# Retention heads of a hybrid decoder step: another plan for the paged sample rows, with key products and key sums at other places in the slot

## The reference

```python
z = h @ w_in            # h = RMSNorm(x); ret_q|ret_k|ret_v|ret_gate|diff_q|diff_k|diff_v|diff_gate
# retention, 4 heads, in chunks of 128 rows with a state S:
inner = einsum('bihd,bjhd->bhij', q, k) * dmask
o     = einsum('bhij,bjhe->bihe', inner, v) + einsum('bihd,bhde->bihe', q * q_dec, S)
S     = gamma**L * S + einsum('bjhd,bjhe->bhde', k * k_dec, v)
# differential attention, 4 heads, two softmax maps of 64 dims each:
a = softmax(s1) - lam * softmax(s2);   o = a @ v
# a sample attends to its cache: 32 pages of 128 positions
past_k = cache_k[page_table];  past_v = cache_v[page_table]
y = x + concat(rms(o_ret) * silu(rg), rms(o_diff) * (1 - lam_init) * silu(dg)) @ w_out
```

## Time and profile before

| | |
|---|---|
| median of 3 runs (lowest, highest) | 1890.08 us (1884.31, 1897.64) |
| the profiled execution | 1889.52 us |
| its span | 1887.7 us |
| granted TensorE clock over the span | 0.937 |
| PE busy | 1633.7 us |
| DVE busy | 1138.0 us |
| POOL busy | 1043.9 us |

### The profile page before, as it was taken

The page is one execution under the profiler, slowest core; times in us unless marked ns, Lnnn a source line. Parts: engine busy times, 40 slices in busy tenths (PEclk is TensorE's granted clock), DMA queues, the critical chain, the costliest instruction groups (busy, mean ns, idle before and its releaser), DMA issues. The chain is left out here.

```text
span 1887.7 us, 28473 instructions
## 1 busy us (share of the span) xinstructions
PE 1633.7 (87%) x8308; PEld 1207.1 (64%) x8308; DVE 1138.0 (60%) x1947; ACT 732.8 (39%) x1947; POOL 1043.9 (55%) x1927
## 2 busy tenths in 40 slices
PE   6869889899888968888999988998988975489999
PEld 1247657576666736676877766876776754366886
DVE  2469677676776635776756978665786753125521
ACT  2333223232232323556655655665554653210000
POOL 4658667767666536787456887556578633200000
PEclk9889999999999979999999999999998996689999
DMA  8764576656548341321025222223233013154441
GB/s 292 251 190 131 165 232 196 207 164 213 188 144 277 118 132 60 90 84 51 23 79 154 82 75 66 68 84 101 88 92 112 24 59 120 56 156 144 145 134 58
DMA packets 169628, 241.00 MB, mean 128 GB/s; under 512 B 15393, under 2 KB 82090, under 8 KB 169458
## 3 DMA queue, kind: packets, MB, share of 16 engines
q1 hardware_dynamic: 137970, 205.55, 34.5%
q10 hardware_dynamic: 28432, 25.21, 4.2%
q0 software_dynamic: 3072, 8.43, 1.1%
HBM read 211.37 MB, written 27.76 MB: 127 GB/s over the span
## 5 line engine op out<-in xcount | busy, mean ns | idle before, releaser
L589 POOL TENSOR_TENSOR s_ring<-s_ring,s_q_row 128x1024 f32<-128x1024 f32 x128 | 316.0, 2485 | 48.7 <-DMA s_ring<-in_cache_k 45.1
L1064 PE MATMUL s_z<-g_w_hi,s_h_hi 128*128 128x512 f32 x512 | 228.4, 446 | 22.3 <-DVE s_h_lo L963 15.8
L1606 PE MATMUL s_z<-g_w_hi,s_h_hi 128*128 128x512 f32 x512 | 225.1, 440 | 24.8 <-DVE s_h_lo L1501 14.3
L1066 PE MATMUL s_z<-g_w_hi,s_h_lo 128*128 128x512 f32 x512 | 206.8, 404 | 0.0
L1065 PE MATMUL s_z<-g_w_lo,s_h_hi 128*128 128x512 f32 x512 | 205.4, 401 | 0.0
L1608 PE MATMUL s_z<-g_w_hi,s_h_lo 128*128 128x512 f32 x512 | 205.2, 401 | 0.0
L1607 PE MATMUL s_z<-g_w_lo,s_h_hi 128*128 128x512 f32 x512 | 204.5, 399 | 0.0
L1350 ACT ACTIVATE s_p<-s_sc,s_neg_max 128x1024 f32<-128x1024 f32 (+4 forms) x192 | 167.0, 874 | 77.0 <-DVE s_neg_max L1531 49.6
L1655 PE MATMUL s_o<-s_v,s_aT 128*128 128x128 f32 x1088 | 168.7, 298 | 15.5 <-ACT s_aT L1331 15.4
L1655 PEld LDWEIGHTS s_o<-s_v,s_aT 128*128 128x128 f32 x1088 | 147.2, 204 | 52.8 <-ACT s_aT L1331 49.2
L963 DVE TENSOR_TENSOR s_h_lo<-g_hT,s_h_hi 128x512 fp32r<-128x512 f32 x128 | 159.0, 1281 | 6.6 <-ACT s_h_hi L854 4.0
(11 more groups left out here) (241 smaller groups left out, 3561.0 us busy)
## 6 DMA issues: line engine op xcount, KB each, us to landing
s_ring<-in_cache_k SPq DMA_DIRECT2D x256, 256.0 KB, 3.0
s_ring<-in_cache_v SPq DMA_DIRECT2D x256, 256.0 KB, 2.9
w_raw<-in_w_in SPq DMA_DIRECT2D x8, 2048.0 KB, 9.8
x_in<-in_x_prompt SPq DMA_DIRECT2D x16, 512.0 KB, 7.0
s_table<-c_rope_ret ACTq DMA_DIRECT2D x64, 128.0 KB, 3.4
s_w_raw<-in_w_in ACTq DMA_DIRECT2D x32, 256.0 KB, 3.6
u_scratch<-s_gate POOLq DMA_DIRECT2D x32, 256.0 KB, 2.6
s_u_in<-u_scratch SPq DMA_DIRECT2D x16, 512.0 KB, 4.8
```

Of the source, the lines that this page charges most:

```text
L589: pool.tensor_tensor(slot[:], slot[:], bc(R.q_row[:].unsqueeze(1), [P, 2, 512]), ALU.mult).then_inc(R.keys_times_q, 1)
L1064: pe.matmul(b[:], hi[:, c, :], g.w_hi[:, wc, :], start=(wc == 0), stop=False)
L1066: last = pe.matmul(b[:], lo[:, c, :], g.w_hi[:, wc, :], start=False, stop=(wc == DC - 1))
L1606: pe.matmul(z_bank[:], hi[:, c, :], g.w_hi[:, wc, :], start=(wc == 0), stop=False)
```

## The change

The plan of the retention stage has other slots. `spread` writes out a slot for each pair or quad, from counts. Row 0 has keys in slots 0 to 5 (2, 3, 3, 3, 3, 2) and values in slots 10 to 16. Rows 1 to 4 end at 17, 29, 41 and 53, 12 slots apart; each has its keys in the 12 slots up to its end and its values in seven slots from end+5, one quad a slot and two in the fourth.

POOL's key products go behind `scale_gates` and `finish` in the slot, and wait until DVE has written both low parts of the slot (`half_low`). DVE's key sums and row steps go from ahead of `mask_inner` to behind `next_state`. `row_stat` gets two buffers; so the wait for the stores of the row before is one row more lenient at end+2, and a wait for them stands at `own`, ahead of the write of `row_own`. The differential stage keeps its plan and its order, and shares the last point.

```diff
-        self.row_stat = sb("row_stat", [HC, 2])
+        self.row_stat = [sb(f"row_stat{i}", [HC, 2]) for i in range(2)]
...
         elif s == end + 2:
             dve.wait_ge(R.row_pe, q + 1)
-            if r >= 1:
-                dve.wait_ge(R.row_stored, 32 * r)
+            if r >= 2:
+                dve.wait_ge(R.row_stored, 32 * (r - 1))
...
         if s == R.own[r]:
             dve.wait_ge(R.values_used, NPAIR // 2 * (r + 1))
+            if r >= 1:
+                dve.wait_ge(R.row_stored, 32 * r)
...
-RET_PLAN = [
-    (list(range(0, 9)), 8, [13, 14, 15, 16, 17, 18]),
-    (list(range(11, 21)), 20, [25, 26, 27, 28, 29, 30]),
-    (list(range(23, 33)), 32, [37, 38, 39, 40, 41, 42]),
-    (list(range(35, 45)), 44, [49, 50, 51, 52, 53, 54]),
-    (list(range(47, 57)), 56, [61, 62, 63, 64]),
-]
+def spread(first, counts):
+
+    return [first + i for i, n in enumerate(counts) for _ in range(n)]
+
+
+RET_VALUES = [1, 1, 1, 2, 1, 1, 1]
+RET_PLAN = [(spread(0, [2, 3, 3, 3, 3, 2]), 5, spread(10, RET_VALUES))] + [
+    (spread(end - 11, [2, 2, 2, 2, 1, 1, 1, 0, 1, 1, 1, 2]), end, spread(end + 5, RET_VALUES))
+    for end in (17, 29, 41, 53)]
...
                 if 0 <= s - 1 < TILES:
                     rotate(s - 1)
-                row_keys_pool(pool, R, s)
                 if s % 2 == 0 and 0 <= (s - 2) // 2 < TILES // 2:
                     scale_gates((s - 2) // 2)
                 done = s - RET_LAG - 2
                 if is_block(done) and done % GROUP == GROUP - 1:
                     finish(done // GROUP)
+                if s in R.keys:
+                    pool.wait_ge(half_low, 2 * s + 4)
+                row_keys_pool(pool, R, s)
                 row_store(pool, io, R, s)
...
                 if is_block(c - 1):
                     gate_output(c - 1)
-                row_keys_dve(dve, R, s - 1)
-                row_steps_dve(dve, g, R, s)
                 if is_block(c):
                     mask_inner(c)
...
                 if is_block(c):
                     next_state(c)
+                row_keys_dve(dve, R, s - 1)
+                row_steps_dve(dve, g, R, s)
                 if k < NH and t == NT - 1:
                     for x in range(DC // 2):
                         split_w(k + 1, x)
```

More of the change, by code:

```diff
@@ L609, in row_steps_dve @@
             dve.wait_ge(R.row_pe, q + 1)
-            if r >= 1:
-                dve.wait_ge(R.row_stored, 32 * r)
-            dve.tensor_reduce(R.row_stat[:, 0:1], R.row_bank[0:HC, 0:P], AX, ALU.max).then_inc(R.row_dve, 1)
+            if r >= 2:
+                dve.wait_ge(R.row_stored, 32 * (r - 1))
+            dve.tensor_reduce(R.row_stat[r % 2][:, 0:1], R.row_bank[0:HC, 0:P], AX, ALU.max).then_inc(R.row_dve, 1)
             dve.wait_ge(R.row_dve, d + 2)
-            dve.tensor_scalar(R.row_diag[:], g.ident[0:HC, 0:HC], R.row_stat[:, 0:1], None, ALU.mult
+            dve.tensor_scalar(R.row_diag[:], g.ident[0:HC, 0:HC], R.row_stat[r % 2][:, 0:1], None, ALU.mult
                               ).then_inc(R.row_dve, 1)
@@ L624, in row_steps_dve @@
             dve.wait_ge(R.row_pe, q + 3)
-            dve.tensor_copy(R.row_stat[:, 1:2], R.row_bank[0:HC, 0:1]).then_inc(R.row_dve, 1)
+            dve.tensor_copy(R.row_stat[r % 2][:, 1:2], R.row_bank[0:HC, 0:1]).then_inc(R.row_dve, 1)
         if s == R.own[r]:
             dve.wait_ge(R.values_used, NPAIR // 2 * (r + 1))
+            if r >= 1:
+                dve.wait_ge(R.row_stored, 32 * r)
             dve.tensor_tensor(R.row_own[:].rearrange("p (h e) -> p h e", e=P),
@@ L680, in row_store @@
             pool.wait_ge(R.row_dve, ROW_DVE * (r + 1))
-            pool.dma_start(io["row_stats"][row:row + 1].rearrange("b s k -> (b s) k"), R.row_stat[:]
+            pool.dma_start(io["row_stats"][row:row + 1].rearrange("b s k -> (b s) k"), R.row_stat[r % 2][:]
                            ).then_inc(R.row_stored, 16)
```

## The result

| | median us (lowest, highest) | ratio to before, 95% interval |
|---|---|---|
| before, 7 executions | 1890.13 (1884.31, 1898.09) | |
| changed, 7 executions | 1901.63 (1896.35, 1906.10) | 1.0059 (1.0035 to 1.0083) |

The changed kernel takes 11.5 us more: slower by 0.6%, where 1% faster was forecast. The time lies within 1% of before, and 1.6 us above the upper end of the range. Its span is 1899.8 us; the granted clock is 0.937, the same as before.

The account below looks back on a forecast made before the run. PE, 87% busy, was taken as the bound, with only its retention-stage stalls to win. Terms of +3.4, -3.7, -6.3, -9.1, -0.5 and -1.9 summed to -18.1 us, for a forecast of 1871 us; range 1842 to 1900.

Parts of the forecast that it names:

- what the change removes: Retention stage: PE's stalls of 27.5 us on `inner_m` and 16.8 us on value pages go.
- Loses twice: Slower rival, slots 20 to 22 of each hand-over: `h_lo` waits through two POOL products, 2.3 us more each; 1912 us, chance 0.20.
- the new waits of PE: Row steps behind two sums end at 8.5 us, PE ready at 6.5: at least 7.6 us a row.
- the 31.7 of the hand-over: Time from the mark of slot 17 at which POOL's products of slot 20 end, in us.
- the hand-over chain: Slots 18 to 21: `q_row`, POOL's products and `finish` delay DVE's step; 36.1 + 0.3 instead of 27.0 us, stall 9.4.
- the 181.0 foretold: Start in us of row 1's first POOL product, after row 0's products end at 175.8 and a 5.2 us gap.
- the row, 103.0 us: A full row of 12 slots: 88.8 us plus hand-over, row-step, `pick_map` and clock terms, 103.0 us.
- my sum: Stage total by stretches: slots 0-17 +3.4, full rows -3.7, -6.3, -9.1, slots 54-63 -0.5, behind slot 63 -1.9; -18.1 us.
- The borders, taken as nothing: Slots 16 and 48 meet one sum a slot; at 32 the `w_lo` wait falls inside the hand-over; no term added.
- The clock, 3 us a row: Each full row loses 3 us to PE's lower clock, the size of the 3.4 us lost in one slot before.
- clock stays up: Faster rival: stalls cut into pieces of about 2 us keep the clock, four times 3 us back; 1859 us, chance 0.10.
- A quad: Two pairs of value pages in a slot cost 0.97 us on top of a bare slot's 6.75 us.

Follow-up runs that it names:

- steps_aligned: Changed kernel with DVE's row steps back ahead of `mask_inner`, each row's end, values and keyless slot one slot later: 1870.4 us, ratio 0.9891.
- q2: Changed kernel with two `q_row` buffers in the retention stage, a semaphore each, nothing else changed: 1907.6 us, ratio 1.0080.
- moved: Changed kernel with key counts of rows 1 to 4 set to 2, 0, 2, 3, 2, 1, 1, 0, 1, 1, 1, 2: 1905.3 us, ratio 1.0077.
- plan_only: Kernel before with the new plan and two `row_stat` buffers, DVE and POOL in their old order: 1881.4 us, ratio 0.9958.

## Why the prediction was wrong, step by step

**Right: what the change removes.** `inner_m` fell to 4.3 us (under 10 was foretold), value waits to 1.0. The mean `h_lo` is 928 ns against 1281 (under 1100 was foretold). "Loses twice" wanted three long waits of `h_lo` a row; the longest one in the stage is 4.43 us, at 196.20, and only one other is over 3 (3.49, at 521.46). So the slower rival came near the measured time by luck: the loss that it priced came from elsewhere.

**Right: the new waits of PE.** Forecast, with the line numbers of the changed kernel: 5 x 1.9 at L643, 4 x 1.8 at L646 and at L649, 4 x 1.4 at L673, 5 x 0.7 at L652, 33.0 us; measured 12.1, 9.0, 6.4, 5.2, 3.8, 36.5 us. (The first 1.9 should read 2.0 by its own terms, 8.5 less 6.5, and the 31.7 of the hand-over 31.6; neither matters.) The sum has them in part inside the hand-over; undoing them gave 31 us (steps_aligned).

**Wrong: the hand-over chain, in size and in what PE waits for.** The 9.4 us were worked out along `q_row`, POOL's products and `finish`, with the row-step waits "contained" in them. POOL's gap between two rows is there, and is longer than I had it: from the end of the last product to the next it takes 6.6 to 7.0 us at the four hand-overs, not 5.2, most of it a wait for the first key pages.

```profile
280.73 4.73 POOL L589 TENSOR_TENSOR s_ring<-s_ring,s_q_row 128x1024 f32<-128x1024 f32 x2 [3.42 <-DVE s_h_lo L969]
...
292.27 2.37 POOL L589 TENSOR_TENSOR s_ring<-s_ring,s_q_row 128x1024 f32<-128x1024 f32 x1 [5.28 <-DMA s_ring<-in_cache_k]
```

(Row 1's first product began at 181.47 us, close to the 181.0 foretold, only because row 0's last one ended 1.3 us early.) Slots 18 to 21 took 40.1 us, not 36.4, a stall of 13.1 us for 9.4. Yet no wait of PE in slots 18 to 22 is on POOL. These are all:

```profile
PE s_row L643 <- DVE s_row_max L607: 2.4, 1, 2.4
PE s_inner L1089 <- ACT s_qkT L878: 1.8, 1, 1.8
PE s_row L646 <- DVE s_row_diag L614: 1.7, 1, 1.7
PE s_row L649 <- DVE s_row_max L622: 1.1, 1, 1.1
PE s_row L652 <- DVE s_row_own L630: 0.7, 1, 0.7
```

They make 7.7 us, and the granted clock of 0.89 over the 48.2 us is at most another 5.3. With `q_row` early (in q2 this gap is 3.9 us) or the products behind the hand-over's `finish` gone (moved) the kernel gained nothing, which fits a POOL chain that is hidden behind the row steps. It is not proof, since both edits also changed what meets the steps. Where the steps are early the second buffer shows: 8 us, seen slot by slot on plan_only alone.

**Mis-sized: the row, 103.0 us.** It measured 105.7, 108.0 and 110.7. From the last mark backwards: my sum puts the mark of slot 63 at 276.5 + 3 x 103.0 + 75.5 = 661.0 us, and it is at 687.5. Of these 26.5 us, 6.2 arise before slot 18 (its start mark is 282.7, not 276.5; slot 16 alone has 4.7 of them), 2.7, 5.0 and 7.7 in the three full rows, 5.0 in the last ten slots. What they consist of overlaps, so the terms below don't add up exactly:

- *The borders, taken as nothing.* Slot 16 took 12.6 us and slot 48 12.0 against 7.85 for their peers, slot 32 3.3 more than slots 20 and 44: 12.2 us. DVE's `w_lo` instructions, two inputs each, meet POOL's product behind `finish`. DVE and POOL ahead of slot 16, and its window:

```profile
262.12 5.92 DVE L974 TENSOR_TENSOR g_w_lo<-s_w_raw,g_w_hi 128x512 fp32r<-128x512 f32 x4
...
263.92 2.36 POOL L589 TENSOR_TENSOR s_ring<-s_ring,s_q_row 128x1024 f32<-128x1024 f32 x1
...
262.10:274.70 12.60, 9.83 (x47) 6.75 (x50) 12.22 (x19) 4.28 (x11) 6.94 (x7) 0.86 0.53 167
```

  Four `w_lo` take 5.92 us; a pair with nothing of POOL's in its way takes 1.28 (at 271.51). PE waited 2.5 us, and at a clock of 0.86 up to another 0.14 x 12.6 = 1.8 were lost. This cost stood in the trace of before, too: slot 16 took 14.0 us there, and slot 48 11.5. The sum starts from bare slots and left it out; it was not brought in by the change. The kernel before, DVE, POOL, window:

```profile
255.06 6.29 DVE L968 TENSOR_TENSOR g_w_lo<-s_w_raw,g_w_hi 128x512 fp32r<-128x512 f32 x2
...
255.02 4.63 POOL L589 TENSOR_TENSOR s_ring<-s_ring,s_q_row 128x1024 f32<-128x1024 f32 x2
...
249.40:263.40 14.00, 9.67 (x46) 6.35 (x42) 13.35 (x17) 4.22 (x12) 10.61 (x13) 0.83 0.80 258
```

- *The clock, 3 us a row.* Length times what is missing from a clock of 1, an upper bound since PE also waits in these stretches, is 5.3, 3.2 and 5.5 us in the three rows: on average 1.7 more than I took. Over the stage it is 23 us before and after. The earlier trace rows Cutting long waits into pieces of about 2 us gave nothing back, against the "clock stays up" rival: slots 20 and 55, with one wait each (1.7 and 2.3 us), ran at 0.84.

```profile
301.80:312.30 10.50, 8.81 (x38) 7.21 (x38) 6.18 (x12) 2.32 (x7) 9.55 (x14) 0.84 0.69 219
615.50:626.40 10.90, 8.56 (x36) 6.71 (x35) 5.68 (x15) 2.31 (x7) 7.26 (x21) 0.84 0.43 135
```

- *A quad.* A slot with one took 7.8 us at full clock with PE never idle, where I had 7.72: 0.13 us by the marks (7.85), thirty times, 4 us.

- *ACT's exponential.* It waits for DVE's step L618, which is now late too, and ACT's copies wait behind it; PE then waits for `qkT`, 10.2 us in six places in all (1.5 before, 2.3 in steps_aligned). The sum has no term for what is queued behind the waiting instruction on ACT.

```profile
315.44 0.42 ACT L659 ACTIVATE s_scores<-s_scores 128x256 f32<-128x256 f32 x1 [2.52 <-DVE s_scores L618]
...
316.71 0.38 ACT L878 COPY s_qkT<-s_turn 128x256 f32<-128x256 f32 x1
```

The other 3.7 us of the miss lie behind slot 63: I expected 1.9 less there, and it is 1.8 more. Over the traces of this document that part took 1204.4 to 1217.7 us, so its cause can't be read from one execution.

The sign hung on this: PE's waits for `inner_m` and value pages fell by 39.0 us and those for `h_lo` by 3.4, while those on row steps rose by 36.5, on `qkT` by 8.7, on POOL's rotation by 4.3 and on `w_lo` by 0.7. The two sides nearly cancel, with 7.8 us left on the wrong side, and the row that I priced at 103.0 us came out 2.7 to 7.7 us longer.

## What to carry to other kernels

When a reduction or product is moved behind other work, don't move with it the small step that another engine waits for: here taking it back, with the one-slot shift that this needs, gave 31 us, more than the 18 that the whole change was forecast to give. Before a step moves, list the engines that wait for it, and for each what stands behind that wait (ACT's copies here). A plan for loads and the orders that free the buffers are one design: the same two orders cost 20 us with one plan and 97 with the other, and one pair of pages a row in the wrong slot 21. And a sum that starts from a bare slot must add back the slots that are long already: the borders were, before the change.

## What the runs showed of the hardware

An 8x8 `tensor_scalar` of DVE whose scalar comes from a tile took 4.53 us while POOL's two 128x1024 products ran (q2); in the changed kernel the median of its eight instances is 0.22 us and the longest 0.97. So size is no protection, and the wait lasted across both products, as in the earlier trace rows. It is not always so long: in the earlier trace rows an `h_lo` got in between two products and took 1.07 us. And it need not end with the products: the `h_lo` at 196.20 us of the changed kernel took 4.43 us, and POOL ran the rest of a pair of products (to 199.26) and two `rotate` instructions meanwhile.

The Trainium skill, "SBUF — State Buffer", section "Who interferes with whom", has a VectorE instruction contend with a GpSimd one that reads SBUF when it has two SBUF inputs, and a `tensor_scalar` when it runs in one of its two-port modes. The trace bears out that this step, with its matrix and its scalar, contends; on which of the two grounds, no run here tells. The section has the shared ports held for one whole instruction; the trace shows a loser that waits for two.
